# A two-part transformer kernel: the helper steps between the input products in another order, a filter output in four banks, the values copied at once, a norm from a VectorE sum

## The reference

```
px = hx @ w_in[i]                       # 1024 -> 1792: q, k, v, fourier input, hyena input
q = rope2d(rmsnorm_2(q, g_q)); k = rope2d(rmsnorm_2(k, g_k))
attn = blocked_attention(q, [kc, k], [vc, v])
four = fft2(f over tokens and each 64 columns).real @ w_fourier
h = sin(fr1 * (z @ w1 + b1)); h = sin(fr2 * (h @ w2 + b2)); h = h @ w3     # hyena filter
two = [h_fwd * decay, 0, reversed h_bwd * decay];  two / sum(|two|, axis=0)
hy = x0 * (longconv(x1 * v, two) + bias)
x = x + ga1 * rmsnorm([attn, four, hy] @ w_out);  then a gated feed-forward part
```

## Time and profile before

| | |
|---|---|
| median of three runs | 2511.07 us |
| profiled execution | 2509.16 us, its span 2507.4 us |
| TensorE busy | 2359.0 us, 94% of the span |
| VectorE, ScalarE, GpSimd busy | 64%, 41%, 28% |
| mean granted TensorE clock | 0.982 |
| high half of a weight, ScalarE (L1469) | 1058 ns |
| low half, VectorE (L1947) and GpSimd (L2269) | 761 ns and 1680 ns |
| input stage, start of the pair to the Fourier output: context, main 1, main 2 | 740.84 to 807.13, 1121.94 to 1242.91, 1817.63 to 1939.53 us |

### The profile page before, as it was taken

One profiled execution on the slowest core, in us unless ns is written; L12 is line 12 of the kernel. 1 busy time (PEld: TensorE's weight loads), 2 busy tenths in 40 slices (PEclk: granted clock), 3 DMA queues, 4 the chain that ended last, 5 costly groups with the idle time before them and its releaser, 6 DMA issues.

```text
span 2507.4 us, 35322 instructions
## 1 busy us (share of the span) xinstructions
PE 2359.0 (94%) x12086; PEld 1837.5 (73%) x12086; DVE 1613.6 (64%) x2706; ACT 1019.9 (41%) x1665; POOL 704.7 (28%) x438
## 2 busy tenths in 40 slices
PE   8999889999889899989999999999899999999998
PEld 5767567676578699966766788888667567888886
DVE  8775588774586577454575476776555754776665
ACT  4344533345434466443252444442233433434421
POOL 3211034211133346621101333334211013233342
PEclk9999999999999999989999999999999999999999
DMA  5412124412143245541210234446512102344464
GB/s 213 170 60 70 65 101 172 151 43 68 51 172 124 71 143 180 179 160 51 84 51 1 93 134 151 143 144 233 186 64 92 51 1 93 116 144 151 142 223 146
DMA packets 81104, 293.98 MB, mean 117 GB/s; under 512 B 9009, under 2 KB 10450, under 8 KB 79028
## 3 DMA queue, kind: packets, MB, share of 16 engines
q1 hardware_dynamic: 80948, 292.03, 34.1%
HBM read 289.90 MB, written 2.10 MB: 116 GB/s over the span
## 4 chain that ended last, share of the span: by engine, by line
PE 51%; DVE 2%; issue 1%; ACT 1%; DVEq 0%; ACTq 0%
PE banks L1140 6%; PE banks L1144 6%; PE banks L1146 6%; PE banks L1163 3%; PE banks L1162 3%; PE banks L1169 3%; PE banks L874 3%; PE banks L875 3%; PE banks L879 3%; PE banks L1035 2%; PE banks L1065 2%; PE banks L1054 2%; PE banks L891 1%; PE banks L896 1%; PE banks L892 1%
## 5 line engine op out<-in xcount | busy, mean ns | idle before, releaser
L1469 ACT ACTIVATE wh_t<-ring 128x1024 fp32r<-128x1024 f32 x264 | 279.0, 1058 | 481.6 <-PE banks L1146 298.0
L1947 DVE TENSOR_TENSOR wl_t<-ring,wh_t 128x512 fp32r<-128x512 f32 x264 | 200.6, 761 | 276.2 <-ACT wh_t L1469 271.5
L2269 POOL TENSOR_TENSOR wl_t<-ring,wh_t 128x512 fp32r<-128x512 f32 x132 | 221.5, 1680 | 542.5 <-ACT wh_t L1469 521.1
L2307 POOL TENSOR_TENSOR wl_t<-ring,wh_t 128x512 fp32r<-128x512 f32 x132 | 236.3, 1790 | 420.1 <-ACT wh_t L1469 420.0
L2236 POOL TENSOR_TENSOR wl_t<-ring,wh_t 128x512 fp32r<-128x512 f32 x72 | 122.5, 1704 | 469.9 <-ACT wh_t L1227 454.0
L1144 PE MATMUL banks<-xh_t,wl_t 128*128 128x512 f32 (+1 forms) x960 | 203.0, 354 | 0.0
L1140 PE MATMUL banks<-xh_t,wh_t 128*128 128x512 f32 (+1 forms) x960 | 203.0, 354 | 0.0
L1146 PE MATMUL banks<-xl_t,wh_t 128*128 128x512 f32 (+1 forms) x960 | 203.0, 354 | 0.0
L1162 PE MATMUL banks<-gh_t,wh_t 128*128 128x512 f32 (+1 forms) x528 | 180.6, 354 | 1.0 <-ACT wh_t L1469 1.0
L1163 PE MATMUL banks<-gl_t,wh_t 128*128 128x512 f32 (+1 forms) x528 | 180.3, 354 | 0.0
L1144 PEld LDWEIGHTS banks<-xh_t,wl_t 128*128 128x128 f32 x960 | 161.4, 189 | 24.9
(11 more groups left out here) (376 smaller groups left out, 4705.1 us busy)
## 6 DMA issues: line engine op xcount, KB each, us to landing
ring<-w_d SPq DMA_DIRECT2D x338, 512.0 KB, 4.0
m_t<-wmod_d SPq DMA_DIRECT2D x160, 512.0 KB, 3.5
qh_t<-tables_d SPq DMA_DIRECT2D x6, 1024.0 KB, 5.3
m_t<-tables_d SPq DMA_DIRECT2D x6, 1024.0 KB, 7.3
par<-p_d SPq DMA_DIRECT2D x4, 696.0 KB, 6.2
x_t<-x_in_d SPq DMA_DIRECT2D x4, 512.0 KB, 6.8
big<-tables_d SPq DMA_DIRECT2D x2, 1024.0 KB
out_d<-x_t SPq DMA_DIRECT2D x4, 512.0 KB, 2.8
```

The costliest lines, as they stand in the source:

```text
L1469: nc.scalar.activation(WH[j % 2], slot2(j), ACT.Copy).then_inc(sm2["w2_hi"], 1)
L1947: nc.vector.tensor_tensor(WL[j % 2][:, 512:1024], slot2(j)[:, 512:1024], WH[j % 2][:, 512:1024].bitcast(F32), ALU.subtract).then_inc(sm2[" ...
L2269: pool.tensor_tensor(WL[j % 2][:, 0:512], slot2(j)[:, 0:512], WH[j % 2][:, 0:512].bitcast(F32), ALU.subtract).then_inc(sm2["w2_lo_a"], 1)
L2307: pool.tensor_tensor(WL[q % 2][:, 0:512], slot2(24 + q)[:, 0:512], WH[q % 2][:, 0:512].bitcast(F32), ALU.subtract).then_inc(sm2["w2_lo_a"], 1)
```

## The change

The filter steps move to later places among the input products, and the order of some head steps with them; the filter output and the Fourier input use the four banks 4 to 7, one for each block; the value transposes go to one bank, with one signal and one copy; the absolute sum of the filter over blocks is one VectorE reduce into a new tile `HABS`, and the norm's matmuls sum that tile over the lanes into bank 5; ScalarE's Abs is gone. `fourier_in` waits for the copied values, the inverse norm and the last spectrum.

```diff
-        ... v2_ready=blocks, v2_copied=blocks,
+        ... v2_ready=1, v2_copied=1,
-                ZT=big[0:33, 26 * n:27 * n], H12=big[0:64, 27 * n:28 * n],
+                ZT=big[0:33, 26 * n:27 * n], HABS=big[:, 26 * n:26 * n + 256], H12=big[0:64, 27 * n:28 * n],
+                VNEW=VCS[:, 0:LC] if is_ctx else VALL[:, LC:LC + T], W=LC if is_ctx else LC + T,
...
 TensorE
                 def head_turn(i):
                     pe.wait_ge(*at2("hn_normed", i + 1))
-                    if i == 0:
-                        pe.wait_ge(*at2("flt_inv", 1))
-                    else:
+                    if i:
                         pe.wait_ge(*at2("hn_turned", i))
...
                 def filter_out():
                     pe.wait_ge(*at2("flt_sin", 2))
                     for b in range(B):
-                        if b >= 2:
-                            pe.wait_ge(*at2("flt_decayed", b - 1))
-                        pe.matmul(ps[4 + b % 2][:], v["H12"][:, b * P:(b + 1) * P], par2[0:64, P_W3:P_W3 + 512],
+                        pe.matmul(ps[4 + b][:], v["H12"][:, b * P:(b + 1) * P], par2[0:64, P_W3:P_W3 + 512],
                                   start=True, stop=True).then_inc(sm2["flt_h"], 1)
                 def filter_norm():
                     pe.wait_ge(*at2("flt_abs", 1))
                     for i in range(2):
-                        for b in range(B):
-                            for d in range(2):
-                                mm = pe.matmul(ps[3][:, i:i + 1], v["HF"][b][:, d * 256 + i * P:d * 256 + (i + 1) * P], ones[:, 0:1],
-                                               start=b + d == 0, stop=b == B - 1 and d == 1)
+                        mm = pe.matmul(ps[5][:, i:i + 1], v["HABS"][:, i * P:(i + 1) * P], ones[:, 0:1], start=True, stop=True)
                     mm.then_inc(sm2["flt_norm"], 1)
...
                 def values2():
+                    pe.wait_ge(*at2("flt_decayed", B))
+                    pe.wait_ge(*at2("acc2_0_free", 1))
+                    pe.sem_inc(waits_passed, 1)
                     for b in range(B):
-                        pe.wait_ge(*at2("v2_copied", b - 1)) if b >= 2 else pe.wait_ge(*at2("flt_decayed", B))
-                        pe.wait_ge(*at2("acc2_0_free", 1))
-                        pe.sem_inc(waits_passed, 1)
-                        pe.transpose(ps[4 + b % 2][:, 0:P], PX2[0][:, b * P:(b + 1) * P], ident).then_inc(sm2["v2_ready"], 1)
+                        mm = pe.transpose(ps[4][:, b * P:(b + 1) * P], PX2[0][:, b * P:(b + 1) * P], ident)
+                    mm.then_inc(sm2["v2_ready"], 1)
                 def fourier_in():
                     pe.wait_ge(*at2("acc2_0_free", 4))
                     pe.wait_ge(*at2("acc2_1_free", 4))
+                    pe.wait_ge(*at2("v2_copied", 1))
+                    pe.wait_ge(*at2("flt_inv", 1))
+                    pe.wait_ge(*at2("spec_copied", B))
                     for b in range(B):
-                        bank = ps[6 + b % 2]
-                        pe.wait_ge(*at2("four_copied", b - 1)) if b >= 2 else pe.wait_ge(*at2("spec_copied", B))
+                        bank = ps[4 + b]
...
+                between = {1: [lambda: filter_layer(0)], 3: [lambda: filter_layer(1), lambda: head_sum(0)],
+                           5: [filter_out, lambda: head_sum(1)], 6: [values2, lambda: head_sum(2)],
+                           7: [lambda: spectrum(0), lambda: head_sum(3)],
+                           8: [lambda: spectrum(1), lambda: head_turn(0), lambda: head_sum(4)],
+                           9: ([lambda: spectrum(2)] if B > 2 else []) + [filter_norm, lambda: head_turn(1)],
+                           10: ([lambda: spectrum(3)] if B > 2 else []) + [lambda: head_turn(2)],
+                           11: [fourier_in, lambda: head_turn(3)], 12: [lambda: head_turn(4)]}
...
 ScalarE
-                def filter_abs():
-                    act.wait_ge(*at2("flt_sums", 1))
-                    nc.scalar.activation(big[:, 14 * n:14 * n + 512 * B], big[:, 14 * n:14 * n + 512 * B], ACT.Abs).then_inc(sm2["flt_abs"], 1)
+                between = {1: [lambda: filter_sin(0)], 2: [lambda: head_square(0)],
+                           3: [lambda: filter_sin(1), lambda: nc.scalar.preload_act_table_set(LNEXP), lambda: head_square(1)],
+                           4: [lambda: head_square(2), lambda: head_rstd(0)], 5: [lambda: head_square(3), lambda: head_rstd(1)],
+                           6: [lambda: head_square(4), lambda: head_rstd(2)],
+                           7: [lambda: spec_copy(0), lambda: head_rstd(3)], 8: [lambda: spec_copy(1), lambda: head_rstd(4)],
+                           9: [lambda: spec_copy(2)] if B > 2 else [], 10: [lambda: spec_copy(3)] if B > 2 else []}
...
 VectorE
-                        nc.vector.tensor_tensor(v["HF"][b], ps[4 + b % 2][:], v["DEC"][b], ALU.mult).then_inc(sm2["flt_decayed"], 1)
+                        nc.vector.tensor_tensor(v["HF"][b], ps[4 + b][:], v["DEC"][b], ALU.mult).then_inc(sm2["flt_decayed"], 1)
...
+                def filter_abs():
+                    nc.vector.tensor_reduce(v["HABS"], big[:, 14 * n:14 * n + 512 * B].rearrange("p (g c) -> p c g", c=256), AX_X, ALU.add,
+                                            apply_absolute_value=True).then_inc(sm2["flt_abs"], 1)
...
                 def values2():
-                    for b in range(B):
-                        dve.wait_ge(*at2("v2_ready", b + 1))
-                        nc.vector.tensor_copy(v["V"][v["V0"] + b], ps[4 + b % 2][:, 0:P]).then_inc(sm2["v2_copied"], 1)
+                    dve.wait_ge(*at2("v2_ready", 1))
+                    nc.vector.tensor_copy(v["VNEW"], ps[4][:, 0:n]).then_inc(sm2["v2_copied"], 1)
...
+                between = {1: [lambda: filter_arg(0)], 3: [lambda: filter_arg(1)], 4: [lambda: head_norm(0)],
+                           5: [filter_decay, lambda: head_norm(1)], 6: [values2, lambda: head_norm(2)],
+                           7: [filter_abs, lambda: head_norm(3)], 8: [lambda: head_turn(0), lambda: head_norm(4)],
+                           9: [filter_inv, lambda: head_turn(1)], 10: [lambda: head_turn(2)], 11: [four_copy, lambda: head_turn(3)],
+                           12: [lambda: head_turn(4)]}
```

More of the change, by code:

```diff
@@ L107, in counts2 @@
         xs2=16, xl2=16, acc2=80, acc2_0_free=40, acc2_1_free=40, down_used=20,
-        hn_squared=5, hn_summed=5, hn_normed=5, turn_ready=5, hn_turned=5, v2_ready=blocks, v2_copied=blocks,
+        hn_squared=5, hn_summed=5, hn_normed=5, turn_ready=5, hn_turned=5, v2_ready=1, v2_copied=1,
         flt_in=2, flt_arg=2, flt_sin=2, flt_h=blocks, flt_decayed=blocks, flt_sums=1, flt_abs=1, flt_norm=1,
@@ L316, in view2 @@
                 V=[VCS[:, i * P:(i + 1) * P] for i in range(b)] if is_ctx else [VALL[:, i * P:(i + 1) * P] for i in range(6)],
-                V0=0 if is_ctx else LC // P, W=LC if is_ctx else LC + T,
+                VNEW=VCS[:, 0:LC] if is_ctx else VALL[:, LC:LC + T], W=LC if is_ctx else LC + T,
                 tiles=[(i, j, half) for i in range(b) for j in range(4) for half in range(2)],
@@ L1025, in scores @@
                         pe.wait_ge(*at2("hn_turned", 5))
-                        pe.wait_ge(*at2("v2_copied", B))
+                        pe.wait_ge(*at2("v2_copied", 1))
                         pe.wait_ge(*at2("md_ready", 1))
@@ L1981, in filter_decay @@
                     ins.then_inc(sm2["flt_sums"], 1)
+                def filter_abs():
+                    nc.vector.tensor_reduce(v["HABS"], big[:, 14 * n:14 * n + 512 * B].rearrange("p (g c) -> p c g", c=256), AX_X, ALU.add,
+                                            apply_absolute_value=True).then_inc(sm2["flt_abs"], 1)
                 def filter_inv():
                     dve.wait_ge(*at2("flt_norm", 1))
-                    link(nc.vector.tensor_scalar(ninv[:], ps[3][:, 0:2], float(n), None, ALU.mult))
+                    link(nc.vector.tensor_scalar(ninv[:], ps[5][:, 0:2], float(n), None, ALU.mult))
                     nc.vector.reciprocal(ninv[:], ninv[:]).then_inc(sm2["flt_inv"], 1)
@@ L2011, in four_copy @@
                         dve.wait_ge(*at2("four_ready", b + 1))
-                        nc.vector.tensor_copy(v["FG"][b], ps[6 + b % 2][:]).then_inc(sm2["four_copied"], 1)
+                        nc.vector.tensor_copy(v["FG"][b], ps[4 + b][:]).then_inc(sm2["four_copied"], 1)
                 def conv_sides(i, taps, which, dst):
@@ L2020, in conv_sides @@
                     dve.sem_inc(sm2[f"acc2_{i % 2}_free"], 1)
-                between = {0: [lambda: filter_arg(0)], 1: [lambda: filter_arg(1)], 2: [filter_decay, lambda: head_norm(0)],
-                           3: [filter_inv], 4: [lambda: head_turn(0), lambda: head_norm(1)],
-                           5: [values2, lambda: head_norm(2)], 6: [lambda: head_turn(1), lambda: head_norm(3)],
-                           7: [lambda: head_turn(2), lambda: head_norm(4)],
```

(3 more changed lines are left out.)

## The result

The changed kernel takes 2481.16 us (median of 4, 2479.08 to 2482.17) beside 2509.40 of the kernel before (median of 4, one more than ahead of the prediction, 2506.66 to 2512.61): ratio 0.9886, 95% interval 0.9869 to 0.9903, so 28 us less. The forecast was 2487, range 2479 to 2499. The profiled run took 2481.09, its span is 2479.3.

The account below looks back on a forecast made before the run. TensorE's queue was taken to bound the kernel, with idle gaps and half clock behind them. Main passes 19.7 plus context 4.5 gave 24.2 us off 2509.16, 2485.0, or 2486.9 as median; range 2479 to 2499.

Parts of the forecast that it names:

- Filter output without a gap: Main passes, idle before filter output to norm: later steps and four banks remove idle and half clock, 6.5 and 6.3 us.
- Norm: Main passes: 32 one-column records become 4, and 28 fewer save 3.05 us on TensorE's path.
- Reduce: VectorE's new sum over 2048 elements a lane: 2.5 us, at most 5, with 0 effect on the end.
- Values: Value transposes in one bank: the third's 0.37 us wait and slow restart go, 0.4 us saved.
- Main passes: Main 1 and main 2: filter output, norm and values sum to 9.9 and 9.8 us saved, 19.7 together.
- Context: Context pass: 8.8 us of idle, low clock and norm records go, 4.3 of waits come back, net 4.5 saved.
- All else: The span outside the context pass and both main passes: forecast difference 0.
- A: Rival: gaps go but the clock doesn't come back, perhaps from 64-row output matmuls; 9.6 us given back, 2496.5; chance 0.09.
- B: Rival: ScalarE's order, sine and load ahead of weights 4 and 6, makes new gaps in all passes; 2496.5 us; chance 0.08.
- C: Rival: Square needs another ScalarE function set; counted as still faster than before; chance 0.08.
- D: Rival, slower: SyncE lands weight 14 late, holding convolution 13 and TensorE's Fourier product; 2518.6 us at 32 us landing; chance 0.03.
- E: Rival: a bank or wait still serialises, gaps only move, norm alone gains 7.5 us or less; 2504 to 2511; chance 0.07.

Follow-up runs that it names:

- e5: Kernel before with six unused 256-column matmuls filling the gap ahead of the third filter output: 2506.59 us, ratio 0.9988.
- e2: Kernel before with four banks for the filter output alone, all steps in their old places: 2505.40 us, ratio 0.9990.
- e4: Changed kernel with the old norm (ScalarE's Abs and 32 one-column records) back, at the new place: 2494.63 us, ratio 0.9941.
- e1: Kernel before with the norm's change alone (VectorE reduce, 4 records) in the old norm's place: 2511.49 us, ratio 1.0015.
- e12: Changed kernel with the old one-column norm split, 16 records behind product 9 and 16 behind product 10: 2488.63 us, ratio 0.9921.
- e10: Changed kernel with VectorE's reduce done twice in each pass, the first result unused: 2481.94 us, ratio 0.9898.
- e7: Changed kernel with the context pass alone reordered (head sums, logarithms, values later; head turns in two banks): 2481.24 us, ratio 0.9886.
- e11: Kernel before with four filter-output banks and the reduced norm read one product later, other filter steps unmoved: 2495.21 us, ratio 0.9942.
- e9: Changed kernel with the old norm's 32 records back, each matmul given 128 columns instead of one: 2491.36 us, ratio 0.9926.

## Why the prediction was right, and where it was not

**Filter output without a gap, -6.5 and -6.3.** Right in size. In main 1 2.72 us of idle went, the sine's 0.44 too, and the clock stayed whole. But the step said that the clock comes back because the gap goes, and that is half of it. e5 and e2 removed the gap and kept the norm, and product 5 lost 1.6 and 2.5 us; e4 shows the same with no idle in the pass. e1 removed the norm's block and kept the gap, and the outputs stayed slow. The clock's 3.3 us in each main pass belong to both edits together: neither is enough. In the kernel before the norm's block stood close behind the gap's slow stretch, and no second fall shows; I read that as "only behind the gap". Why the block lowers nothing there, no run shows. I priced each edit from a trace in which the other's effect hid it. The sum held since the change makes both; so far as the step priced them one by one, that it came out right was luck.

**Norm, -3.05 for 28 records.** 3.14 (e12 beside the change). But without it (e4) 14.0 us are lost in the trace, where its records alone, with 1.4 in the context pass, make 7.6: main 1 is 6.4 longer, main 2 5.5 and the stretch between them 2.1. The 1.4 us of the context pass are not there: with its records back that pass takes the same time, since TensorE waits later instead.

**Reduce.** Mis-sized, 3.77 us where I took 2.5, within the bound of 5. That it is covered in its new place was right (e10), though the row named for it, 3.76 of 15 us busy, is of the old place; there it was a wait of 2.07, 1.47 and 4.45 (e1). In the change it runs at 1170.82, and the norm that reads it stands at 1192.84.

**Values, -0.4.** The transposes take 0.60, and the wait of 0.37 is gone; 0.73 saved from spacing (1.17 before, 0.44 after). Fourier input and its new waits: 0 in the main passes, right.

**Main passes, 9.9 and 9.8 against 10.95 and 10.7.** The idle time counts 3.5, the records 3.1, the clock 3.3; the last microsecond lies in part in the values (0.73 for 0.4); the rest was not followed.

**Context, 4.5 against 3.3.** The mechanism was right but for the norm's 1.4, with waits where the walk put them: 0.51 at the second layer (said: hardly), 0.81 and 1.53 in front of head sums 0 and 1 (0.65, 0.8), 1.28 and 0.90 at turns 2 and 4 (1.0, 0.9). Missed was 0.99 at the values, which wait for the last decay. The idle sum is 6.0 where I had 4.3; of the 0.5 that I allowed for a bank behind product 13, nothing shows. e7 shows that most of these waits could go, and that it would not have helped.

**All else, 0 against -3.2.** 2.8 of it lies between the context pass and main 1. That stretch as a whole, kernel before, then e2, then changed:

```profile
807.13:1121.94 314.81, 287.01 (x2108) 262.65 (x2106) 185.87 (x399) 163.01 (x298) 150.19 (x98) 0.96 0.44 145
805.11:1117.16 312.05, 283.38 (x2109) 260.06 (x2107) 186.03 (x399) 162.82 (x298) 150.29 (x98) 0.97 0.46 146
803.57:1115.56 311.99, 283.55 (x2108) 259.46 (x2106) 185.40 (x399) 162.99 (x298) 150.33 (x97) 0.97 0.45 146
```

This is half clock that shifted, as the range allowed for. The four banks alter nothing where there are two blocks, so up to main 1 e2 runs what the kernel before runs, and it takes 312.05 us there. The 2.8 us are a difference between executions of the same instructions, and no step of the change is shown to make it.

**Rivals.** A, clock doesn't come back: false for the output matmuls (1.00 after), but its idea, that something other than the gap lowers the clock, is what e4 showed; I had named the wrong matmuls. B, ScalarE makes gaps: false in the main passes (no idle at all), in context part of the 2.9 us. C, Square needs another function set: false; two loads stand in each pass as before (three of each line), though Square now runs between two sines. So the trace answers, for the sine's set, what the Trainium skill, "ScalarE: Activation LUTs", section "Table sets: the hidden batching unit", leaves open by not naming square. D, SyncE: false; weight 14 went out 1.1 us behind the tables, and TensorE has no idle time in either main pass. E, the gaps only move: false in the main passes, where none is left.

## What to carry to other kernels

Price edits that remove idle time and edits that remove tiny matmuls together, not one by one. Here both lowered the clock, the first fix moved the loss to the second cause, and each alone measured +3.5 and -2.6 us where both together gave -14 (e1, e2, e11). An unbroken block of one-column matmuls cost its own time and then up to 3.3 us of the product behind it (e4). Let a vector engine do the first part of such a sum, well ahead of where it is read, or at least break the block up (e12: 5 to 6 us for nothing but that). And after shortening a stage, read the granted clock everywhere else before you count the gain.

## What the hardware showed that was not expected

With TensorE busy without a gap, the granted clock was still 0.59 behind 32 one-column records (e4, over 7 us of main 1), and 1.00 behind the same 32 with 128 columns in 3.73 us (e9), and behind two blocks of 16 (e12). The reduce that reads 2048 elements a lane with a stride takes 3771 ns, 1.84 ns an element, where one of 768 elements from PSUM takes 1.23 (948 ns); the two differ in length and in memory too, so the stride's part isn't shown. And a context pass 4.4 us shorter left the whole kernel's time as it was (e7).
